# Two-layer trunk on one Trainium2 core: the mixer's output product split by k, six of eight contraction chunks moved into the RWKV tail

## The reference, cut to what matters

```
h = h + 0.5 * rms_norm(swiglu(rms_norm(h)))     # first feed-forward part
m = token_mix(rms_norm(h))                      # the mixer
h = h + rms_norm(m)
h = h + 0.5 * rms_norm(swiglu(rms_norm(h)))     # second feed-forward part

def token_mix(xn):
    ...                                          # projections, attention (512 channels),
    ...                                          # causal convolution (256), RWKV recurrence (256)
    merged = concat([rms_norm(o_a, gn_a), rms_norm(o_b, gn_b), rms_norm(o_c, gn_c)])
    return merged @ w_out                        # 1024 x 1024

def rwkv_output(o, r, k, v, gate):               # the last of the three to be ready
    o = layer_norm(o, w, b)                      # per head of 64
    o = o + sum(r * k * rk) * v                  # the bonus
    return o * gate
```

## Time and profile before

| | us |
|---|---|
| median of three runs | 2822.65 |
| the three runs | 2815.61, 2822.67, 2822.65 |
| the profiled execution | 2825.52 |
| span of its trace, first to last instruction | 2823.7 |
| PE busy in it | 2587.2 |
| DVE busy | 1411.1 |
| ACT busy | 847.4 |

### The profile page before, as it was taken

How to read it: one execution, slowest core, us unless ns; L and a number is a source line. 1 busy time by engine, 2 the same in 40 slices (tenths; PEclk the granted TensorE clock), 3 DMA queues, 4 the chain that set the end, 5 groups by cost and what they waited for, 6 DMA issues and landing times.

```text
span 2823.7 us, 52595 instructions
## 1 busy us (share of the span) xinstructions
PE 2587.2 (92%) x22567; PEld 2453.4 (87%) x22567; DVE 1411.1 (50%) x2053; ACT 847.4 (30%) x1516; POOL 34.3 (1%) x36
## 2 busy tenths in 40 slices
PE   7999999978978799999989999999788787899998
PEld 6999998967748689999989999898666587899997
DVE  3444227846756564442264442376476455644423
ACT  4222223134411342222242222331343113422222
POOL 0000000000000000000000000000100000000000
PEclk9999999988878899999999999999878798999999
DMA  3333334330020123333223333341301002233332
GB/s 102 89 90 96 90 87 116 75 91 15 4 57 3 54 68 89 89 95 91 86 73 89 89 91 92 90 112 50 105 1 40 21 9 71 75 89 89 92 91 72
DMA packets 409310, 206.85 MB, mean 73 GB/s; under 512 B 51476, under 2 KB 407614, under 8 KB 409072
## 3 DMA queue, kind: packets, MB, share of 16 engines
q1 hardware_dynamic: 409152, 204.55, 25.5%
HBM read 197.86 MB, written 11.30 MB: 74 GB/s over the span
## 4 chain that ended last, share of the span: by engine, by line
PE 82%; DVE 12%; ACT 4%; issue 1%; DMA 0%; DVEq 0%; SPq 0%; ACTq 0%
PE ps L546 20%; PE ps L550 19%; PE ps L547 19%; PE ps L1413 2%; PE ps L321 2%; PE ps L288 2%; PE ps L1289 2%; PE ps L322 2%; PE ps L323 2%; PE ps L1391 1%; PE ps L1374 1%; PE ps L361 1%; DVE rstd L456 1%; PE ps L1613 1%; PE ps L1861 1%
## 5 line engine op out<-in xcount | busy, mean ns | idle before, releaser
L546 PE MATMUL ps<-xnH,wH 128*128 128x260 f32 x3232 | 847.0, 283 | 8.3 <-DVE wL L535 4.9
L547 PE MATMUL ps<-xnL,wH 128*128 128x260 f32 x3232 | 841.4, 282 | 0.0
L550 PE MATMUL ps<-xnH,wL 128*128 128x260 f32 x3232 | 650.6, 283 | 0.0
L546 PEld LDWEIGHTS ps<-xnH,wH 128*128 128x128 f32 x3232 | 610.2, 189 | 12.0 <-ACT rstd L401 5.9
L547 PEld LDWEIGHTS ps<-xnL,wH 128*128 128x128 f32 x3232 | 608.1, 188 | 0.3
L535 DVE TENSOR_TENSOR wL<-nat,wH 128x1024 fp32r<-128x1024 f32 (+1 forms) x332 | 389.5, 1195 | 425.0 <-ACT wH L531 424.6
L550 PEld LDWEIGHTS ps<-xnH,wL 128*128 128x128 f32 x3232 | 498.0, 188 | 0.0
L531 ACT ACTIVATE wH<-nat 128x1024 fp32r<-128x1024 f32 (+1 forms) x332 | 342.7, 1035 | 393.8 <-DMA nat<-in_ffn_down 181.4
L547 PE MATMUL ps<-actL,wH 128*128 128x260 f32 x1296 | 338.7, 283 | 0.0
L546 PE MATMUL ps<-actH,wH 128*128 128x260 f32 x1296 | 338.7, 283 | 0.0
L550 PE MATMUL ps<-actH,wL 128*128 128x260 f32 x1296 | 261.0, 282 | 0.0
(11 more groups left out here) (357 smaller groups left out, 3539.8 us busy)
## 6 DMA issues: line engine op xcount, KB each, us to landing
nat<-in_ffn_gate SPq DMA_DIRECT2D x88, 512.0 KB, 3.7
nat<-in_ffn_up SPq DMA_DIRECT2D x88, 512.0 KB, 3.7
nat<-in_ffn_down SPq DMA_DIRECT2D x64, 512.0 KB, 3.6
nat<-in_w_in SPq DMA_DIRECT2D x36, 512.0 KB, 3.7
nat<-in_ffn_down SPq DMA_DIRECT2D x32, 384.0 KB, 3.2
big<-in_cmp_w SPq DMA_DIRECT2D x8, 512.0 KB, 7.7
nat<-in_w_in SPq DMA_DIRECT2D x16, 256.0 KB, 3.3
nat<-in_w_out SPq DMA_DIRECT2D x32, 128.0 KB, 2.9
```

Of the source, the lines that this page charges most:

```text
L546: pe.matmul(out, wH[:, slot(u), k, :], xh[:, k0 + k, t], start=first and k == 0, stop=False)
L547: pe.matmul(out, wH[:, slot(u), k, :], xl[:, k0 + k, t], start=False, stop=False)
L550: ins = pe.matmul(out, wL[:, slot(u), k, :], xh[:, k0 + k, t], start=False, stop=last and k == nk - 1)
```

## The change

w_out is taken in two parts. For each of the eight output tiles, chunks 0 to 5 of the contraction (KE = 6) form units 90 to 97, now with 6 x 128 columns each; chunks 6 and 7 of all tiles are two further units, 98 and 99, each with four tiles by two chunks. The second feed-forward part starts at unit 100.

- The high and low parts of chunks 0 to 5 are made during the RWKV inverse: ACT after its second akv copy, DVE between the steps of the inverse (one chunk in each of four steps, two in the last). mL now takes the place of `merged`.
- Units 90 and 91 are loaded before the recurrence's state is stored, and split by ACT in the inverse and by DVE at the start of the tail.
- PE computes tiles 0 to 2 over chunks 0 to 5 (`pe_wout_early`) between the first and the second gvar, tiles 3 to 7 after the second. ACT copies each to fT (`act_wout_early`).
- `pe_wout_late` waits for all eight copies and for chunks 6 and 7, and computes them tile by tile in three pairs of banks; DVE adds each to fT (`dve_wout_add`), ACT squares it from fT. Tiles 6 and 7 go by halves. The split of unit 101 stands in DVE's list after the add of tile 5.

```
-U_IN, U_OUT, U_END = 68, 90, 166
+U_IN, U_OUT, U_END = 68, 90, 168
+KE = 6
...
-        mH = over("mH", at_a, 0, [P, KC, TOK], F32R)
-        mL = over("mL", at_a, (FC + 7) * TOK, [P, KC, TOK], F32R)
+        mH = [over("mHa", at_a, 6144, [P, 4, TOK], F32R)[:, c, :] for c in range(4)]
+        mH += [v[:, c, :] for v in (over("mHb", at_a, 9264, [P, 2, TOK], F32R), over("mHc", at_a, 0, [P, 2, TOK], F32R))
+               for c in range(2)]
+        mL = over("mL", at_x, 0, [P, KC, TOK], F32R)
...
         def act_out_half(act, e, h):
...
+            if e % 3 == 2:
+                for m in range(full(e), KC):
+                    act.wait_ge(S("fb_out"), 10 * (e // 3) + 2 * h + m + 1)
+                    act.wait_ge(S("sq_added"), adds_before(e) + m - 2)
+                    act.activation(sq[:, m % 2, half(h)], f_v[:, m, half(h)], ACT.Square).then_inc(S("fq_ready"), 1)
+                return
...
+            sp.wait_ge(S("mat_mm"), at("mat_mm", 4))
+            sp_wout(sp, l, 0, 2)
             for m in range(2):
                 sp.wait_ge(S("swk_ready"), at("swk_ready", m + 1))
...
+            act.wait_ge(*stage("bonus_in"))
+            act_merged_hi(act, 0, KE)
+            for m in range(2):
+                act_unit(act, U_OUT + m, KE)
             act.wait_ge(S("wu_mm"), at("wu_mm", 1))
...
                 if n == 0:
                     dve_bonus_in(dve, T, link)
                     continue
+                dve_merged_lo(dve, n - 1, n + n // 5)
                 for m in range(2):
                     dve.wait_ge(S("dx_mm"), at("dx_mm", 2 * (n - 1) + m + 1))
...
             ins.then_inc(S("gvar"), 1)
+            pe.wait_ge(S("bonus_used"), at("bonus_used", 1))
+            pe_wout_early(pe, 0, 3)
             pe.wait_ge(S("gsq"), at("gsq", 2))
-            for m in range(2):
-                ins = mm_tokens(pe, 4, ones, tr[:, m, :], m == 0, m == 1)
+            pe.wait_ge(S("groot"), at("groot", 1))
+            for m in range(2):
+                ins = mm_tokens(pe, 0, ones, tr[:, m, :], m == 0, m == 1)
             ins.then_inc(S("gvar"), 1)
+            pe_wout_early(pe, 3, KC)
 
         def act_rw_out(act, T, link):
-            act.wait_ge(S("o_mm"), at("o_mm", 2))
-            act.wait_ge(*stage("attn_done"))
-            act_merged_hi(act, 0, 3)
             act.wait_ge(*stage("g_centered"))
             link(act.activation(tr, oT, ACT.Square))
             act.sem_inc(S("gsq"), 1)
-            act_merged_hi(act, 3, 6)
+            act_unit(act, U_OUT + 2, KE)
             act.wait_ge(S("gvar"), at("gvar", 1))
...
             act.wait_ge(S("wkv_st"), at("wkv_st", 64))
-            for u in OUT_UNITS[0:2]:
-                act_unit(act, u)
+            act_unit(act, U_OUT + 3, KE)
+            act_wout_early(act, 0)
+            act_unit(act, U_OUT + 4, KE)
+            act_wout_early(act, 1)
             act.wait_ge(*stage("oc_ready"))
             link(act.activation(tr, oT, ACT.Square))
             act.sem_inc(S("gsq"), 1)
+            act_unit(act, U_OUT + 5, KE)
+            act_wout_early(act, 2)
             act.wait_ge(S("gvar"), at("gvar", 2))
...
         def dve_rw_out(dve, T, link):
-            dve.wait_ge(S("o_mm"), at("o_mm", 2))
-            dve_merged_lo(dve, 0, 2)
+            for m in range(2):
+                dve_unit(dve, U_OUT + m, KE)
             dve.wait_ge(S("gmean"), at("gmean", 1))
...
+                ins = dve.tensor_tensor(halves(oB[:, m, :]), pair(4 + 2 * m), halves(xm[:, 4 + m, :]), ALU.mult)
+            ins.then_inc(S("bonus_used"), 1)
+            dve.wait_ge(S("bonus_used"), at("bonus_used", 1))
+            dve_unit(dve, U_OUT + 2, KE)
             dve.wait_ge(S("groot"), at("groot", 1))
...
             link(ins)
-            link(dve.tensor_tensor(oT, oT, wdec, ALU.add))
+            dve_unit(dve, U_OUT + 3, KE)
+            link(dve.tensor_tensor(oT, oT, oB, ALU.add))
             link(dve.tensor_tensor(oT, oT, gate, ALU.mult))
             dve.sem_inc(reach("oc_ready"), 1)
-            dve_merged_lo(dve, 5, 6)
-            for u in OUT_UNITS[0:2]:
-                dve_unit(dve, u)
+            dve_unit(dve, U_OUT + 4, KE)
+            dve_unit(dve, U_OUT + 5, KE)
             dve.wait_ge(S("groot"), at("groot", 2))
...
+                    sp.dma_start(nat[:, slot(u), 4:KE, :], w[:, 512:768, m * P:(m + 1) * P]
+                                 .rearrange("a (k p) n -> p (a k) n", p=P)).then_inc(S(f"nat_full{slot(u)}"), 16)
+                else:
+                    b = nat[:, slot(u), :, :].rearrange("p (k m) n -> p k m n", k=2)
+                    for k in range(2):
+                        sp.dma_start(b[:, k], w[:, (KE + k) * P:(KE + k + 1) * P, (m - KC) * 512:(m - KC + 1) * 512]
+                                     .rearrange("a p (m n) -> p (a m) n", n=P)).then_inc(S(f"nat_full{slot(u)}"), 16)
...
+        def pe_wout_early(pe, first, last):
+
+            for m in range(first, last):
+                if m >= 2:
+                    pe.wait_ge(S("fa_out"), at("fa_out", m - 1))
+                pe_unit(pe, U_OUT + m, 4 + 2 * (m % 2), mH, mL, nk=KE, wait_x="ml_ready" if m == 0 else None)
+
+        def act_wout_early(act, m):
+            act.wait_ge(S("unit_done"), count(U_OUT + m + 1, None))
+            act.activation(halves(f_v[:, m, :]), pair(4 + 2 * (m % 2)), ACT.Copy).then_inc(S("fa_out"), 1)
+
+        def pe_wout_late(pe, e):
+
+            def tile(m, h):
+
+                u = U_OUT + KC + m // 4
+                for k in range(2):
+                    ins = pe_products(pe, u, 4 * k + m % 4, 2 * (m % 3), h, mH, mL, KE + k, k == 0, k == 1)
+                return ins
+
+            def start(m):
+
+                if m % 4 == 0:
+                    pe.wait_ge(S("lo_ready"), count(U_OUT + KC + m // 4 + 1, None))
+                if m >= 3:
+                    pe.wait_ge(S("fb_out"), 10 * (e // 3) + m - 2)
+
+            pe.wait_ge(S("ml_ready"), at("ml_ready", KC))
+            pe.wait_ge(S("fa_out"), at("fa_out", KC))
+            pe.wait_ge(S("groot"), at("groot", 2))
+            for m in range(full(e)):
+                start(m)
+                tile(m, 0)
+                ins = tile(m, 1)
+                if m == 3:
+                    ins.then_inc(S("unit_done"), 1)
+                else:
+                    ins.then_inc(S("fb_mm"), 1)
+            for m in (6, 7):
+                start(m)
+                tile(m, 0).then_inc(S("fb_mm"), 1)
+            tile(6, 1).then_inc(S("fb_mm"), 1)
+            pe_out_sums(pe, e, 0)
+            tile(7, 1).then_inc(S("unit_done"), 1)
+            pe_out_sums(pe, e, 1)
...
+            b = 2 * (m % 3)
+            if h is None:
+                v, p = halves(f_v[:, m, :]), pair(b)
+            else:
+                v, p = f_v[:, m, half(h)], ps[:, b + h, 0:HALF]
+            dve.tensor_tensor(v, v, p, ALU.add).then_inc(S("fb_out"), 1)
+
+        def act_wout(act, e):
+
+            act_unit(act, U_OUT + 6, KE)
+            act_wout_early(act, 3)
             act.wait_ge(*stage("merged_ready"))
             act_merged_hi(act, 6, KC)
...
+            for m in range(4, KC):
+                act_unit(act, U_OUT + m + 3, size_of(U_OUT + m + 3))
+                act_wout_early(act, m)
+            for m in range(full(e)):
+                if m == 4:
+                    act_unit(act, U_UP[1] + 1)
+                act.wait_ge(S("fb_out"), 10 * (e // 3) + m + 1)
+                if m >= 2:
+                    act.wait_ge(S("sq_added"), adds_before(e) + max(1, m - 2))
+                act.activation(sq[:, m % 2, :], f_v[:, m, :], ACT.Square).then_inc(S("fq_ready"), 1)
+            act_end(act, e)
+
+        def dve_wout(dve, e):
+
+            dve_unit(dve, U_OUT + 6, KE)
             dve_merged_lo(dve, 6, KC)
...
+            for m in range(4, KC):
+                dve_unit(dve, U_OUT + m + 3, size_of(U_OUT + m + 3))
+            for m in range(full(e)):
+                dve_wout_add(dve, e, m)
+                if m >= 2:
+                    dve_add_square(dve, e, m - 1)
+                if m == 5:
+                    dve_unit(dve, U_UP[1] + 1)
+            dve_add_square(dve, e, full(e) - 1)
+            for h in range(2):
+                for m in (6, 7):
+                    dve_wout_add(dve, e, m, h)
```

More of the change, by code:

```diff
@@ L147 @@
[L147 to L151, removed]
@@ L320, in pe_products, with pe_out_end @@
             out, t = ps[:, bank + h, 0:HALF], half(h)
[L321 to L325, removed]
+            xh, xl = (xh[kx] if xh is mH else xh[:, kx, :])[:, t], xl[:, kx, t]
+            pe.matmul(out, wH[:, slot(u), k, :], xh, start=first, stop=False)
+            pe.matmul(out, wH[:, slot(u), k, :], xl, start=False, stop=False)
+            return pe.matmul(out, wL[:, slot(u), k, :], xh, start=False, stop=last)
+        def pe_out_end(pe, e, units):
             for h in range(2):
                 for i, (u, m, k0, nk) in enumerate(units):
-                    ends = m == KC - 2 or i == 1
```

(28 more changed lines are left out.)

168 lines of the change are left out of this document (81 added, 87 removed).

## The result

The changed kernel takes 2796.72 us (median of 5 runs, 2785.75 to 2798.89) against 2822.65 us (5 runs, 2815.46 to 2823.98): a ratio of 0.9904, 95% interval 0.9888 to 0.9920. That is faster; 2801.7 was forecast, with 2792 to 2812 as the range. The profiled execution is the one of 2796.72 us, 28.8 less than the profiled execution before (2825.52).

A forecast was written before the change was run, and what follows sets the result against it. PE was taken as the bound, busy 2587.2 of 2823.7 us, with gains only where it idles and the end waits. Both layers -25.25, clock +2.6 and +1.7: -20.95, from the median 2822.65 to 2801.7 us; range 2792 to 2812.

The forecast's parts named there:

- first reciprocal: Layer 0, closing norm behind the output product: reciprocal of the first half at 996.3 us, where it stood at 1009.05.
- stage, layer 0: Layer 0, from the state output to the first reciprocal of the closing norm, 75.98 us before: -12.75 us.
- stage, layer 1, low rate paid once: Layer 1, state output to first reciprocal, 76.83 us before: -11.9 us, with one 1.7 us low-rate charge for PE's pause.
- Work into idle time: Between the two gvar sums: three six-chunk tiles, 13.0 us, all fall into PE's 14.19 us of idle time.
- The stall before the late part: After the five tiles: PE waits 1.05 us for the last copy, behind unit 100's split in ACT's list.
- DVE's order at the end: End of the late part: unit 101's split (1.22 us) precedes the sums, tile 7's second half add (0.4) the reciprocal.
- The inverse: RWKV inverse: DVE's low parts are hidden except in the last step, where two subtractions add 1.1 us per layer.
- The clock: PE's granted clock: 1.7 us for the 2.1 us pause in one layer of two, 2.6 at layer 1's entry.
- the rival in which every pause is paid: Both layers pay the low rate before second gvar and late part, layer 1 also at its entry: 2807 us; chance 0.17.
- the one in which none is: Rival: no new PE pause costs time at the low rate, 2797 us; chance 0.08.
- The entry: First to second reciprocal behind the tail: -0.54 us per layer for ACT's dropped copies, plus 2.6 low rate in layer 1.
- The slow rival: Output product runs at 1.2 GHz from first tile to the sums, tiles taking 8.64 us: 2885 us; chance 0.03.

The follow-up runs named there:

- the four edits: Changed kernel with four early tiles between the sums, late wait relaxed, unit 101's split and last half add moved, low parts of chunks 4 and 5 moved: 2786.22, again 2778.28 us.

## Why the prediction was right, point by point

Each step is counted from the end of the first gvar (941.26 before, 940.37 after).

| step | forecast | measured |
|---|---|---|
| second gvar starts | 15.1 | 15.01 |
| five tiles end | 38.7 | 38.65 |
| late part starts | 39.8 | 39.87 |
| first reciprocal | 55.0 | 55.05 |
| stage, layer 0 | -12.75 | -12.73 |
| stage, layer 1, low rate paid once | -11.9 | -12.09 |
| inverse, each layer | +1.1 | +0.88 |
| entry, layer 0 | -0.54 | -1.56 |
| entry, layer 1 | +2.06 | +1.16 |

- *Work into idle time.* Right, and shown by the runs with no tiles, with useless products and with four tiles between the sums.
- *The stall before the late part.* Forecast 1.05, measured 1.22, with the cause that was named; taking the wait away took it off.
- *DVE's order at the end.* That the add of the last half tile and the split of unit 101 set the end was read from the lists alone; moving both gained 1.76 us.
- *The inverse.* Right in place and nearly in size.
- *The clock.* The charge of one pause of 2.1 us in two was a guess between rows, and its size was 1.7. In the six kernels that keep this pause (the changed one, its repeat and the runs with useless products, without the late wait, with the split later and with the low parts later) it was paid in 3 of 12 places, at 1.5 us: layer 1 twice and layer 0 once. The two profiles of the changed kernel as it stands paid it in the same layer. So the rival in which every pause is paid falls, and the one in which none is does too; that the first profile paid just one of its two, as charged, is partly luck. The Trainium skill, TensorE: Matmul & The Clock Gate, section "HAM oscillation — how this bites in real kernels", has waits between groups of matmuls bring the low rate back, and the waits of its example are longer than 2.1 us. The trace agrees for the 15 us pause and for the one of 4.2 us in the entry; the 3 of 12 came after a shorter one, so here the measurement decides.
- *The entry.* The term that was mis-sized: I let layer 0 keep both its low stretches and charged layer 1 the same 2.6. Each layer paid some 1.6 of that, 18.21 and 18.34 us where a clean entry has 17.18 - 0.54 = 16.64, and the repeat paid the same (18.16 and 18.34). That size has luck in it: the run with the low parts later, with the same lists from the tail on, took 20.00 and 20.02 us, at a lower clock. What decides it is open. Layers 0 and 1, first the changed kernel, then that run:

```profile
995.42:1013.63 18.21, 10.83 (x58) 8.96 (x58) 12.50 (x28) 8.30 (x20) 0.00 (x0) 0.91 0.10 29
2370.67:2389.01 18.34, 10.96 (x58) 9.09 (x58) 12.49 (x27) 8.31 (x20) 0.00 (x0) 0.91 0.10 30
```

```profile
985.29:1005.29 20.00, 13.31 (x57) 11.35 (x58) 12.57 (x27) 8.09 (x19) 0.00 (x0) 0.75 0.09 26
2360.89:2380.91 20.02, 13.31 (x57) 11.35 (x58) 12.57 (x27) 8.09 (x19) 0.00 (x0) 0.75 0.10 28
```

- *The slow rival.* The tiles run at 1.00 throughout; it falls.

The terms sum to -12.73 - 12.09 + 2 x 0.88 - 1.56 + 1.16 = -23.5 in the profiled execution, where -20.95 was forecast. The other 5.3 of its 28.8 us lie outside the mixer's ends: the three entries that the change doesn't touch took 105.4 us in the profile of before and 99.1 in that of after, 6.3 less, and the rest about 1 us more. The long stretches of the last section, which vary most, happen to be equal in the two profiles (835.4 and 835.6 us). Two executions of the changed kernel already differ by 2.2 us in those entries (99.1 and 101.3). Whether the rest is chance as well is not shown: all eleven profiles with the change have 99.1 to 103.1, and of before there is only one. The medians differ by 25.9 us.

## What to carry to other kernels

Where a chain across engines leaves the busiest one idle, ask which part of the next product needs nothing from that chain; splitting the contraction there is worth the idle time that it fills, and nothing by itself. Then read each engine's list for what stands ahead of the last wait on the path: a wait that asked for more than it needed and a few instructions in the wrong place cost 0.9 to 1.8 us per layer each here. The stage behind an edit belongs in the reading too: TensorE's rate alone moved the next stage between 18.2 and 20.3 us here, as much as some of the edits gained.

## What the runs showed of the hardware

Pauses filled with matmuls whose results are thrown away kept the granted clock at 2.4 GHz and shortened a stretch of waits between three engines by up to 3.35 of 20.17 us. Where the entry's first pause (3.6 to 4.2 us) was left empty, in ten profiles with the change, part of the entry ran at 1.2 GHz in all 20 places; after the pause of 2.1 us it happened in 3 of 12.

Most of the spread between two executions of one kernel can come from a stage that no edit touched: of the 12.6 us between the two profiles with the four edits (2789.6 and 2777.0), 10.7 lie in it. From the last reciprocal of the entry into the mixer to the first mask of the inverse it took between 403.5 and 419.5 us with the same instructions, by the granted clock:

```profile
1830.83:2250.35 419.52, 358.91 (x2699) 310.76 (x2699) 270.08 (x446) 126.53 (x322) 13.53 (x15) 0.85 0.21 55
```

```profile
1830.14:2233.69 403.55, 342.94 (x2699) 298.23 (x2699) 269.82 (x447) 126.00 (x322) 13.54 (x15) 0.89 0.22 57
```

The first is layer 1 of the changed kernel, the second that of the run with the split of unit 101 later: PE is busy 15.97 us longer in the first, and the stretch is 15.97 us longer. Over the 24 such stretches of the twelve profiles the length follows the time at 1.2 GHz with a correlation of 0.996. What starts the one or the other is open.
